# RWKV-7 scan: the order in which four engines take its steps

## The chip, the core and the metric

The kernel runs on one core of a Trainium2 chip. The metric is the device time of one execution in microseconds (us). Engines: TensorE (PE; its weight loads are PEld), VectorE (DVE), ScalarE (ACT), GpSimd (POOL) and SyncE (SP), which issues the DMAs.

## The reference, cut to what matters

A trunk of two layers is run on 128 context tokens and 512 latent tokens with the same weights. The second layer mixes tokens by a bidirectional RWKV-7 scan: 16 heads of 64 channels, a state of 64 x 64 per head and direction.

```python
def rwkv7_scan(r, w, k, v, kk, a, s0):
    def step(s, inp):
        r_t, w_t, k_t, v_t, kk_t, a_t = inp
        sa = jnp.einsum('bhvk,bhk->bhv', s, -kk_t)
        s = s * w_t[:, :, None, :] + sa[..., None] * (kk_t * a_t)[:, :, None, :] + v_t[..., None] * k_t[:, :, None, :]
        return s, jnp.einsum('bhvk,bhk->bhv', s, r_t)
...
    def direction(d, s0):
        w_log = -jax.nn.softplus(-(w0[d] + jnp.tanh(xw @ w1[d]) @ w2[d]).astype(jnp.float32)) - 0.5
        decay = heads(jnp.exp(-jnp.exp(w_log)))
        a = heads(jax.nn.sigmoid((a0[d] + (xa @ a1[d]) @ a2[d]).astype(jnp.float32)))
        kd = k * (1 + (a - 1) * k_a_h)
...
        bonus = jnp.sum(r * kd * r_k_f, axis=-1, keepdims=True) * v
        return y, bonus, s_fin
...
    yn = ((y - mu) * lax.rsqrt(var + LN_X_EPS)).reshape(bsz, n_tok, D_MODEL) * ln_w + ln_b
    out = (yn + (bonus_f + bonus_b).reshape(bsz, n_tok, D_MODEL)) * g
    return out.astype(h.dtype) @ wo, (s_f, s_b)
```

Here kk is the normalised key, mu and var are the mean and variance of y over a head, and g is a gate.

## The kernel before, in words

**Tiling.** Tokens lie along the free dimension (640: 512 latent, 128 context), channels on the 128 partitions, so one tile of 128 channels holds a **pair** of heads. There are 8 pairs, q = 0 to 7. Of a pair the 640 tokens are taken in five **iterations** of 128 tokens (two chunks of 64), both directions at once: iteration n belongs to pair n // 5, and NB = 40 of them run. Within a chunk the recurrence is solved in matrix form, between chunks the state is carried.

**Steps of a chunk solve.** For block m (the work of iteration m, made some iterations ahead):

- G (gram): TensorE makes the products of keys with keys in banks 0 and 1; VectorE masks them out of there (L2490, L2492); GpSimd adds the identity (L2615).
- A1, A2, A3: squares, fourths and eighths of that matrix; ScalarE copies the first two (L2376, L2380), GpSimd adds the identity (L2622), VectorE reads A3 out of the same banks 0 and 1 (L2505, L2506), and the next block's G waits for that.
- GR (read_keys): products of keys with reads in banks 6 and 7, masked by VectorE (L2499).
- B1, B2, B3, B4, B5: the block inverse. ScalarE copies B1 and B2 (L2384, L2388, L2392), VectorE adds B3, B4 and B5 (all L2510). BT turns keys (L2242), ScalarE copies it (L2398). B0 is GpSimd's copy of values (L2641).

**Steps of the walk.** For each of the two chunks of an iteration, s = 0 and 1: x (TensorE, then VectorE's sum L2520), u (TensorE, then ScalarE's copy L2404), s (TensorE, then VectorE's state update L2531, or L2529 where a direction ends; GpSimd prepares its decayed half, L2607, which its table calls x0 and x1). The next chunk's x needs the updated state. y1 is ScalarE's copy of the outputs (L2413); x0 of the next iteration needs it, for the bank.

**Once for a pair.** On ScalarE: decays0 to decays4 (L2370 to L2372, one for each iteration), the sigmoids "prompt", "w", "a" (L2323, L2325), k_square (L2357), k_sum, mean (L2344), var (L2351, L2352), final (L2341), bonus, state (L2335). On VectorE: cum0, cum1 (L2446, L2447), keys0 (L2456, L2460), keys1, keys2, keys3 (L2464, L2467, L2470), staging0 to staging4 (L2476 to L2479), bonus_raw (L2567, L2568), values (L2548), y_sum (L2552), mean (L2541), y_norm0 (L2560, L2561), y_norm1 (L2564), gate (L2544), k_sum (L2451). On TensorE: the head sums of k_sum, mean, var and bonus, the gate product, the transposes of values (L2133), state and final, and the LoRA products of prompt, w and a. These side products share banks 6 and 7 with GR and BT; each waits until the one before it has been read out.

**What sets the order.** Every engine runs its queue in order and waits on semaphores. The order in a queue is written by hand, in one table for each engine: PE_ORDER, DVE_ORDER, ACT_ORDER, POOL_ORDER, and PE_FIRST and ACT_FIRST for the first iteration of a pair (n = 0, 5, ..., 30). run_iteration (from L2033) walks a table for n from -4 to 41. An entry is a step, or a step with an offset:

```python
                what, ahead = entry if isinstance(entry, tuple) else (entry, 0)
                m = n + ahead
```

so ("B5", 0) in iteration n and ("B5", 1) at the end of iteration n - 1 give nearly the same queue. A step that is done once for a pair is in the table of every iteration and runs only when m has the right remainder by 5 (ASIDE and aux). Behind each iteration up to 34 (VectorE: 35) a call of out_ahead_act or out_ahead_dve splits one tile of the next stage's input into a high and a low part (out_high L1144, out_low L1148; six tiles, iterations 29 to 34 on ScalarE, one later on VectorE); in the last iterations the entry "ahead" does that, and on TensorE it runs products of the next stage.

Of the kernel before, what the change touches and what calls it, by code (L numbers as in the profile page):

```python
# [115 lines left out]
def program(nc, a, o):  # L116
    with ExitStack() as ctx:
# [73 lines left out]
        V, A, G = nc.vector, nc.scalar, nc.gpsimd  # L191
# [28 lines left out]
        for l in range(LAYERS):  # L220
            if l == 0:
                ada_stage(0)
                w = a["ab_w_in"][0]
# [241 lines left out]
        fast_x0, x0 = {}, 0  # L465
# [1361 lines left out]
        QD, A1, A2, DD = blocks4(2), blocks4(2), blocks4(3), blocks4(2)  # L1827
# [171 lines left out]
        def place(q, c):  # L1999
# [1 line left out]
            return c if c < 8 else c + 2 * (q % 2)  # L2001


        PE_ORDER = ("var", "mean", "B5", ("final", -1), ("s1", -1), ("GR", 1), ("B1", 1), "x0", ("A1", 2), "bonus", "a", "u0", "state", ("B2", 1), "w", ("A2", 2),
                     "prompt", "s0", ("B3", 1), ("BT", 1), "x1", ("A3", 2), ("values", 1), ("B4", 1), ("gate", 1), ("k_sum", 1), "u1", ("G", 3))
        def with_ahead(order, after):
            return tuple(x for entry in order for x in ((entry, "ahead") if entry in after else (entry,)))

        PE_LAST = {NB - 2: with_ahead(PE_ORDER, ("s0", "x1", "u1")), NB - 1: with_ahead(PE_ORDER, (("s1", -1), "x0", "u0", "s0", "x1", "u1"))}
        PE_FIRST = ("B5", "var", ("s1", -1), ("values", 2), ("GR", 1), ("B1", 1), ("A1", 2), "prompt", ("bonus", 1), "x0", "u0", ("B2", 1), ("A2", 2), "w", "s0", ("A3",  # L2010
                     2), ("a", -1), ("B3", 1), ("k_sum", 1), "x1", ("mean", -1), ("gate", 2), ("BT", 1), ("B4", 1), "final", ("state", 1), "u1", ("G",
                     3))
        DVE_ORDER = (("bonus_raw", -1), "B3", ("staging0", -1), ("x1", -1), ("A3", 1), "values", ("keys1", -1), "B4", "gate", "k_sum", ("G", 2), "mean", ("keys2", -1),
                     ("s1", -1), "B5", ("GR", 1), "y_sum", "x0", "staging3", "staging4", "staging1", "y_norm0", "keys3", ("cum0", -1), ("keys0", 1),
                     "cum1", "staging2", "y_norm1", "s0")
        ACT_FIRST = (("k_square", 2), "prompt", "decays3", "u0", ("A2", 2), ("a", -1), "decays1", ("B2", 1), "w", ("BT", 1), ("decays4", 2), "u1", "y1", ("B1", 2),
                     ("decays0", -1), "var", ("decays2", 2), ("state", 2), ("mean", -1), ("A1", 3), ("final", -1), ("bonus", -1), ("k_sum", 2))

        def first_of_pair(n):
            return n >= 0 and n % 5 == 0 and n + 5 < NB  # L2020

        ACT_ORDER = ("a", "state", "bonus", "u0", ("B2", 1), ("A2", 2), ("k_square", 1), ("decays1", 1), ("BT", 1), "mean", ("decays0", 1), "u1", ("decays3", 1), "w",
                     ("k_sum", 1), "final", ("var", 1), "y1", ("decays2", 1), ("decays4", 1), ("B1", 2), ("A1", 3), "prompt")
        POOL_ORDER = (("A2", 3), ("x1", 1), ("G", 4), ("B0", 3), ("x0", 2), ("A1", 4))

        DVE_LAST = with_ahead(DVE_ORDER, ("staging2",))
        ACT_LAST = with_ahead(ACT_ORDER, (("var", 1),))

# [41 lines left out]
        def rwkv_pe(pe):  # L2070
# [224 lines left out]
            for n in range(-4, NB + 2):  # L2295
                run_iteration(n, PE_FIRST if first_of_pair(n) else PE_LAST.get(n, PE_ORDER), tasks, side)
            for item in LAST_ASIDE:
# [4 lines left out]
        def rwkv_act(act, step):  # L2302
# [118 lines left out]
            for n in range(-4, NB + 2):  # L2421
                run_iteration(n, ACT_FIRST if first_of_pair(n) else ACT_LAST if n >= 35 else ACT_ORDER, tasks, side, aux)
                if n < 35:
# [10 lines left out]
        def rwkv_dve(dve, step):  # L2434
# [145 lines left out]
            for n in range(-4, NB + 2):  # L2580
                run_iteration(n, DVE_LAST if n >= 36 else DVE_ORDER, tasks, side, aux)
                if n < 36:
# [439 lines left out]
```

## Time and profile before

| | us |
|---|---|
| median of 3 runs | 2205.68 |
| lowest and highest run | 2205.41 and 2209.05 |
| the profiled execution, its own time | 2206.71 |
| its span, first to last instruction | 2204.9 |
| TensorE busy in the span | 2048.0 (93%) |
| VectorE, ScalarE, GpSimd busy | 1415.6, 1041.6, 317.6 |
| the scan, from its first staging to its last state update | about 1177 to 1703 |

How to read it: busy time counts an engine's instructions; register, branch, semaphore and DMA-issuing instructions are not in it. Times in rows are us from the span's start. A timeline merges like instructions (x is their count) and tells the idle time of the engine before them, with the work that ended it. PEclk is the granted share of TensorE's clock. An instruction's end overlaps the next one's start by up to 0.1 us.

### The profile page before, as it was taken

To read this page: it belongs to the slowest core of one execution; us is meant where nothing else is said; L and a number is where in the kernel's file an instruction comes from. 1 tells how busy PE (TensorE), PEld (TensorE's weight loads), DVE (VectorE), ACT (ScalarE), POOL (GpSimd) and SP (SyncE) were. 2 spreads that over 40 slices of the span, in tenths; PEclk is the share of its full clock that TensorE was granted. 3 is DMA by queue.
4 is the path that set the end of the run, shared out by engine and by line. 5 is a ranking of instruction groups with operands and counts; after the bars stand their busy time and mean duration, and the time that the engine had idled before them with its cause. 6 is when DMAs were issued, how large, how long until landed. Compare 5 with 4: busy or idle time off the path is not lost. (4 is left out here: it accounts for less than half of the span.)

```text
span 2204.9 us, 60453 instructions
## 1 busy us (share of the span) xinstructions
PE 2048.0 (93%) x26203; PEld 1836.3 (83%) x26203; DVE 1415.6 (64%) x2698; ACT 1041.6 (47%) x1887; POOL 317.6 (14%) x542
## 2 busy tenths in 40 slices
PE   5999877898999999989998899999988999999999
PEld 2689754578999999967997777777777989999999
DVE  2242375655666675777535888888885468585857
ACT  5252354434535343566334566666664264434353
POOL 1000131001000000010002544444442200000000
PEclk8999999999999999999998999999999999999999
DMA  7212205960231323113210000000000221322312
GB/s 281 86 39 79 79 1 213 372 226 20 77 96 58 96 66 107 58 29 115 80 39 8 8 10 7 9 9 10 10 25 25 88 66 58 96 77 77 96 58 87
DMA packets 129764, 167.86 MB, mean 76 GB/s; under 512 B 13900, under 2 KB 87388, under 8 KB 129372
## 3 DMA queue, kind: packets, MB, share of 16 engines
q1 hardware_dynamic: 129500, 164.00, 22.2%
q8 instruction: 208, 3.41, 0.6%
q14 instruction: 56, 0.46, 0.1%
HBM read 160.44 MB, written 3.54 MB: 74 GB/s over the span
## 5 line engine op out<-in xcount | busy, mean ns | idle before, releaser
L178 PE MATMUL psum<-arena 64*64 64x64 f32 (+5 forms) x16064 | 585.6, 240 | 94.8 <-ACT arena L1411 14.8
L178 PEld LDWEIGHTS psum<-arena 64*64 64x64 f32 (+3 forms) x16064 | 464.6, 140 | 231.2 <-issue 99.5
L178 PE MATMUL psum<-hidden_high,weights_high 128*128 128x320 f32 x896 | 277.2, 309 | 0.5 <-DVE arena L1020 0.5
L178 PE MATMUL psum<-hidden_low,weights_high 128*128 128x320 f32 x896 | 276.9, 309 | 0.0
L178 PE MATMUL psum<-hidden_high,weights_low 128*128 128x320 f32 x896 | 276.9, 309 | 0.0
L178 PE MATMUL psum<-norm_high,weights_high 128*128 128x320 f32 x960 | 218.8, 309 | 0.0
L178 PE MATMUL psum<-norm_low,weights_high 128*128 128x320 f32 x960 | 218.8, 309 | 0.0
L178 PE MATMUL psum<-norm_high,weights_low 128*128 128x320 f32 x960 | 218.7, 309 | 0.0
L178 PEld LDWEIGHTS psum<-hidden_high,weights_high 128*128 128x128 f32 x896 | 168.2, 188 | 0.9 <-issue 0.7
L178 PEld LDWEIGHTS psum<-hidden_low,weights_high 128*128 128x128 f32 x896 | 168.2, 188 | 0.0
L178 PEld LDWEIGHTS psum<-hidden_high,weights_low 128*128 128x128 f32 x896 | 168.2, 188 | 0.0
L178 PEld LDWEIGHTS psum<-norm_low,weights_high 128*128 128x128 f32 x960 | 160.5, 188 | 0.0
L178 PEld LDWEIGHTS psum<-norm_high,weights_low 128*128 128x128 f32 x960 | 160.5, 188 | 0.0
L178 PEld LDWEIGHTS psum<-norm_high,weights_high 128*128 128x128 f32 x960 | 160.4, 188 | 0.0
L999 DVE TENSOR_TENSOR hidden<-hidden 128x640 f32<-128x640 f32 x32 | 26.4, 826 | 175.6 <-ACT hidden L946 175.6
L944 ACT ACTIVATE hidden<-psum 128x640 f32<-128x640 f32 x64 | 45.1, 705 | 189.0 <-PE psum L178 189.0
L899 ACT ACTIVATE weights_high<-weight_sums 128x512 fp32r<-128x512 f32 x128 | 76.7, 624 | 106.5 <-DVE weight_sums L918 55.6
L621 POOL TENSOR_TENSOR arena<-arena 128x640 f32<-128x640 f32 x24 | 41.7, 1738 | 568.8 <-ACT arena L613 568.1
L1020 DVE SCALAR_TENSOR_TENSOR arena<-psum,ada,arena 128x128 f32<-128x128 f32 (+2 forms) x208 | 83.4, 430 | 30.1 <-PE psum L178 29.3
L903 DVE TENSOR_TENSOR weights_low<-weight_sums,weights_high 128x512 fp32r<-128x512 f32 x128 | 88.3, 700 | 8.4 <-ACT weights_high L899 8.4
L899 ACT ACTIVATE weights_high<-weights 128x512 fp32r<-128x512 f32 x96 | 58.2, 622 | 68.4 <-PE psum L178 68.4
L2615 POOL TENSOR_TENSOR arena<-arena,constants 64x128 f32<-64x128 f32 x160 | 67.2, 420 | 153.0 <-DVE arena L2490 139.9
(268 smaller groups left out, 3992.9 us busy)
## 6 DMA issues: line engine op xcount, KB each, us to landing
weights<-in_mlp_w SPq DMA_DIRECT2D x64, 1024.0 KB, 5.3
arena<-in_ada_w SPq DMA_DIRECT2D x24, 2048.0 KB, 9.3
arena<-in_ab_w_in SPq DMA_DIRECT2D x6, 2048.0 KB, 7.8
arena<-in_ab_w_out SPq DMA_DIRECT2D x2, 2048.0 KB, 9.0
arena<-in_rwkv_wv SPq DMA_DIRECT2D x2, 2048.0 KB, 8.1
arena<-in_rwkv_wr SPq DMA_DIRECT2D x2, 2048.0 KB, 8.1
arena<-in_rwkv_wk SPq DMA_DIRECT2D x2, 2048.0 KB, 7.9
arena<-in_x_sample SPq DMA_DIRECT2D x1, 2048.0 KB, 10.1
```

Of the source, the lines that this page charges most:

```text
L178: return nc.tensor.matmul(out, lhsT, rhs, start=start, stop=stop, skip_group_check=shared)
L621: G.tensor_tensor(total, a0 if k == 1 else total, (a0, a1)[k % 2], ALU.add).then_inc(S("norm_squares_added"), 1)
L899: A.activation(slots_of(WHI)[:, j], slot_raw(l, grp, i, j), ACT.Copy).then_inc(S("slot_high"), 1)
L903: V.tensor_tensor(slots_of(WLO)[:, j], slot_raw(l, grp, i, j), slots_of(WHI)[:, j], ALU.subtract)\
L944: A.activation(h, PS[:, 2 * j:2 * j + 2, 0:HN], ACT.Relu).then_inc(S("up_evacuated"), 1)
L999: V.tensor_tensor(h[:, H_T1:H_T3 + 1, :], h[:, H_B11:H_B22 + 1:3, :], h[:, H_B12:H_B12 + 1, :].broadcast_to([P, 2, HN]), ALU.subtract)\
L1020: ins = V.scalar_tensor_tensor(x, PS[:, bank, c:c + t1 - t0], gate[:, m, g:g + 1], x, ALU.mult, ALU.add)
L2615: ins = G.tensor_tensor(P1[HALF[h], d, 0], QD[r, h, 0], units(r), ALU.add)
```

## The change

The order tables of TensorE, VectorE, ScalarE and GpSimd are replaced by others. The functions that do the steps, their waits, ASIDE, aux and run_iteration are the same.

```diff
-        PE_ORDER = ("var", "mean", "B5", ("final", -1), ("s1", -1), ("GR", 1), ("B1", 1), "x0", ("A1", 2), "bonus", "a", "u0", "state", ("B2", 1), "w", ("A2", 2),
-                     "prompt", "s0", ("B3", 1), ("BT", 1), "x1", ("A3", 2), ("values", 1), ("B4", 1), ("gate", 1), ("k_sum", 1), "u1", ("G", 3))
+        PE_ORDER = ("prompt", "mean", "var", "B5", ("final", -1), ("s1", -1), ("GR", 1), ("B1", 1), "x0", ("A1", 2), "a", "w", "state", "bonus", "u0", ("B2", 1), ("A2",
+                     2), "s0", ("B3", 1), ("BT", 1), "x1", ("A3", 2), ("B4", 1), ("values", 1), ("k_sum", 1), ("gate", 1), "u1", ("G", 3))
...
-        PE_FIRST = ("B5", "var", ("s1", -1), ("values", 2), ("GR", 1), ("B1", 1), ("A1", 2), "prompt", ("bonus", 1), "x0", "u0", ("B2", 1), ("A2", 2), "w", "s0", ("A3",
-                     2), ("a", -1), ("B3", 1), ("k_sum", 1), "x1", ("mean", -1), ("gate", 2), ("BT", 1), ("B4", 1), "final", ("state", 1), "u1", ("G",
-                     3))
-        DVE_ORDER = (("bonus_raw", -1), "B3", ("staging0", -1), ("x1", -1), ("A3", 1), "values", ("keys1", -1), "B4", "gate", "k_sum", ("G", 2), "mean", ("keys2", -1),
-                     ("s1", -1), "B5", ("GR", 1), "y_sum", "x0", "staging3", "staging4", "staging1", "y_norm0", "keys3", ("cum0", -1), ("keys0", 1),
-                     "cum1", "staging2", "y_norm1", "s0")
-        ACT_FIRST = (("k_square", 2), "prompt", "decays3", "u0", ("A2", 2), ("a", -1), "decays1", ("B2", 1), "w", ("BT", 1), ("decays4", 2), "u1", "y1", ("B1", 2),
-                     ("decays0", -1), "var", ("decays2", 2), ("state", 2), ("mean", -1), ("A1", 3), ("final", -1), ("bonus", -1), ("k_sum", 2))
+        PE_FIRST = (("k_sum", 2), "B5", ("s1", -1), ("final", 1), ("state", 1), ("GR", 1), ("B1", 1), ("A1", 2), "prompt", "x0", "u0", ("B2", 1), ("gate", 2), ("mean",
+                     -1), ("A2", 2), "w", ("bonus", 1), "s0", ("var", -1), ("A3", 2), ("B3", 1), "x1", ("BT", 1), ("B4", 1), "u1", ("values", 2),
+                     ("G", 3), ("a", -1))
+        DVE_ORDER = ("k_sum", "values", ("G", 2), "mean", "B5", ("s1", -1), ("keys2", -1), ("GR", 1), ("keys0", 1), "y_sum", "x0", "staging3", ("cum0", -1), "cum1",
+                     "staging4", "staging1", "y_norm0", "keys3", "staging2", "s0", ("B3", 1), "staging0", ("bonus_raw", -1), "x1", "y_norm1", ("A3",
+                     2), "keys1", ("B4", 1), ("gate", 1))
+        ACT_FIRST = (("decays0", -1), ("decays3", 2), ("y1", -1), ("bonus", -1), ("mean", -1), ("a", -1), ("k_square", 2), ("state", 2), ("B1", 1), ("A1", 2), "decays1",
+                     ("decays4", 2), "prompt", "u0", ("A2", 2), "var", ("final", -1), ("k_sum", 2), ("B2", 1), "w", ("BT", 1), "u1", ("decays2", 2))
...
-        ACT_ORDER = ("a", "state", "bonus", "u0", ("B2", 1), ("A2", 2), ("k_square", 1), ("decays1", 1), ("BT", 1), "mean", ("decays0", 1), "u1", ("decays3", 1), "w",
-                     ("k_sum", 1), "final", ("var", 1), "y1", ("decays2", 1), ("decays4", 1), ("B1", 2), ("A1", 3), "prompt")
-        POOL_ORDER = (("A2", 3), ("x1", 1), ("G", 4), ("B0", 3), ("x0", 2), ("A1", 4))
+        ACT_ORDER = (("y1", -1), "decays2", "decays3", ("B1", 1), ("A1", 2), "a", "decays4", "bonus", "u0", "state", ("B2", 1), ("A2", 2), "mean", ("decays1", 1),
+                     ("k_square", 1), ("BT", 1), "prompt", ("decays0", 1), "u1", ("k_sum", 1), "final", "w", ("var", 1))
+        POOL_ORDER = ("G", ("B0", -1), ("x0", -2), "A1", "A2", ("x1", -2))
```

The tables of the last iterations (PE_LAST, DVE_LAST, ACT_LAST) are made from these. Written out as queues, with the number of the block or iteration behind a step, VectorE's from x0 of iteration 17 to x1 of iteration 20 is

```
before: x0.17 y_norm0 keys3 y_norm1 s0.17 B3.18 staging0 x1.17 A3.19 B4.18 gate G.20 s1.17 B5.18 GR.19 x0.18
        staging1 staging2 s0.18 bonus_raw B3.19 x1.18 A3.20 values B4.19 G.21 s1.18 B5.19 GR.20 x0.19
        staging3 staging4 s0.19 B3.20 x1.19 A3.21 B4.20 k_sum G.22 s1.19 B5.20 GR.21 y_sum x0.20 keys0 s0.20 B3.21 x1.20
after:  x0.17 y_norm0 keys3 s0.17 B3.18 staging0 x1.17 y_norm1 A3.19 B4.18 gate G.20 B5.18 s1.17 GR.19 x0.18
        staging1 staging2 s0.18 B3.19 x1.18 A3.20 B4.19 values G.21 B5.19 s1.18 GR.20 x0.19
        staging3 staging4 s0.19 B3.20 bonus_raw x1.19 A3.21 B4.20 k_sum G.22 B5.20 s1.19 GR.21 keys0 y_sum x0.20 s0.20 B3.21 x1.20
```

In the third iteration of a pair keys2 also goes from ahead of s1 and B5 to behind them. ScalarE's changes in a pair are: y1 of the fourth iteration ahead of decays3, decays4 from ahead of B1 and A1 to behind them, u0 of the fifth iteration ahead of state, and mean ahead of BT.

## Rows read from the trace of the kernel before

**Rows 1.** The page, busy us and share of the span of an engine.

```profile
PE 2048.0 (93%) x26203; PEld 1836.3 (83%) x26203; DVE 1415.6 (64%) x2698; ACT 1041.6 (47%) x1887; POOL 317.6 (14%) x542
```

**Rows 2.** Pair 2: us, PE, PEld, DVE, ACT, POOL, PEclk, DMA share, GB/s.

```profile
1325.00:1388.00 63.00, 57.40 (x1905) 48.23 (x1902) 53.92 (x118) 40.06 (x98) 28.61 (x60) 1.00 0.04 10
```

**Rows 3.** Timeline of VectorE in iteration 12: start us, us, instruction, idle before.

```profile
1358.42 1.14 DVE L2564 TENSOR_TENSOR arena<-arena 128x640 f32<-128x640 f32 x1
1359.60 0.47 DVE L2531 SCALAR_TENSOR_TENSOR arena<-psum,arena 128x64 f32<-128x64 f32 x2
...
1362.35 0.41 DVE L2506 COPY arena<-psum 128x256 f32<-128x256 f32 x1
...
1363.01 0.80 DVE L2544 TENSOR_TENSOR arena<-arena,psum 128x640 f32<-128x640 f32 x1
1363.84 0.69 DVE L2490 TENSOR_TENSOR arena<-psum,constants 128x512 f32<-128x512 f32 x1
...
1366.21 1.29 DVE L2499 TENSOR_TENSOR arena<-psum,constants 128x512 f32<-128x512 f32 x2 [0.28 <-PE psum L178]
```

**Rows 4.** Timeline of TensorE, x1 and what follows, iterations 12 and 17.

```profile
1360.13 4.10 PE L178 MATMUL psum<-arena 64*64 64x64 f32 x124 [1.65 <-DVE arena L2531]
...
1422.73 5.70 PE L178 MATMUL psum<-arena 64*64 64x64 f32 x124 [1.65 <-DVE arena L2531]
```

**Rows 5.** Busy time around two falls of the clock, columns as in rows 2.

```profile
1419.90:1423.30 3.40, 1.75 (x67) 1.48 (x66) 3.30 (x7) 1.96 (x5) 1.39 (x2) 1.00 0.02 5
1423.30:1426.70 3.40, 3.40 (x38) 2.20 (x28) 2.39 (x8) 0.00 (x0) 0.00 (x0) 0.50 0.00 0
...
1488.10:1491.50 3.40, 3.40 (x30) 2.14 (x32) 2.55 (x7) 0.00 (x0) 0.00 (x0) 0.50 0.00 0
```

**Rows 6.** Timeline of VectorE in iteration 13, bonus_raw.

```profile
1371.54 0.82 DVE L2567 TENSOR_TENSOR arena<-arena 128x640 f32<-128x640 f32 x1
1372.39 1.15 DVE L2568 SCALAR_TENSOR_TENSOR arena<-arena,param_cols 128x640 f32<-128x640 f32 x1
```

**Rows 7.** Timeline of GpSimd, the sum behind A2 in iterations 13 and 14.

```profile
1371.57 1.28 POOL L2622 TENSOR_TENSOR arena<-arena,constants 128x256 f32<-128x256 f32 x1 [2.07 <-ACT arena L2380]
...
1383.42 0.64 POOL L2622 TENSOR_TENSOR arena<-arena,constants 128x256 f32<-128x256 f32 x1 [1.54 <-ACT arena L2380]
```

**Rows 8.** Timeline of TensorE in iterations 13 and 14.

```profile
1372.91 0.46 PE L178 MATMUL psum<-arena 64*64 64x64 f32 x16 [0.29 <-POOL arena L2622]
...
1375.85 3.01 PE L178 MATMUL psum<-arena 64*64 64x64 f32 x80 [0.24 <-DVE arena L2510]
1379.14 1.43 PE L178 MATMUL psum<-arena 64*64 64x64 f32 x56 [0.28 <-ACT arena L2413]
```

**Rows 9.** Timeline of ScalarE in iteration 14, decays4 and u0.

```profile
1378.78 0.42 ACT L2370 ACTIVATE arena<-arena 128x256 f32<-128x256 f32 x1
...
1381.08 0.55 ACT L2404 ACTIVATE arena<-psum 64x128 f32<-64x128 f32 x2
```

**Rows 10.** VectorE (B3 sum) and TensorE (k_sum head sums), iteration 14.

```profile
1383.67 0.42 DVE L2510 TENSOR_TENSOR arena<-psum,arena 128x256 f32<-128x256 f32 x1
...
1385.34 1.26 PE L178 MATMUL psum<-arena,constants 64*64 64x320 f32 x8
```

**Rows 11.** Timeline of VectorE in iteration 15, x0, keys0 and s0.

```profile
1392.00 0.29 DVE L2520 TENSOR_TENSOR arena<-psum,arena 128x128 f32<-128x128 f32 x1 [0.23 <-DVE arena L2552]
...
1392.38 1.05 DVE L2460 SCALAR_TENSOR_TENSOR arena<-arena,param_cols 128x640 f32<-128x640 f32 x1
1396.19 0.48 DVE L2531 SCALAR_TENSOR_TENSOR arena<-psum,arena 128x64 f32<-128x64 f32 x2 [2.75 <-PE psum L178]
```

**Rows 12.** Timeline of ScalarE ahead of iteration 0, the state copy.

```profile
1195.27 0.34 ACT L2335 ACTIVATE arena<-psum 128x64 f32<-128x64 f32 x2
```

**Rows 13.** Timelines of VectorE (out_low, iteration 32) and TensorE (B4, iteration 33).

```profile
1615.57 0.82 DVE L1148 TENSOR_TENSOR mixed_low<-arena,mixed_high 128x640 fp32r<-128x640 f32 x1
...
1630.92 1.65 PE L178 MATMUL psum<-arena 64*64 64x64 f32 x64 [0.80 <-DVE arena L2510]
```

## The prediction

> **What bounds the kernel now.** I read the page first: TensorE is busy 93% of the span, the other engines far less [rows 1]. The change touches nothing but the four order tables of the RWKV scan, so the next view is the busy time of stretches of the scan, one pair of heads (five iterations) each: in the 63 us of pair 2 TensorE is at work for 57, VectorE for 54, ScalarE for 40, GpSimd for 29 [rows 2]. A pair therefore ends when TensorE has done its fixed work plus its short stalls, and VectorE has only some 9 us of slack in 63. So I read the timelines of the four engines inside pairs and asked of each stall which read-out it waited for.
>
> **What the change really moves.** An entry of a table is a step and an offset in iterations, and only the resulting row of steps on each queue counts. Written out that way, GpSimd's queue comes out the same, step by step. TensorE's has two swaps in a pair: the second block (B4) ahead of the value transposes, the state transposes ahead of u0. ScalarE's has four in a pair. VectorE's is the one that changes: in each of 39 iterations the third block's sum (B5) goes ahead of the state update s1, and in each pair y_norm1, bonus_raw, values and keys0 change places. In the last pairs the six splits of the next stage's input (out_high, out_low) shift too, since they hang at the end of an iteration. No instruction and no DMA is added or removed; SyncE's queue stays.
>
> **B5 ahead of s1.** TensorE makes B5 before s1, so the sum can run while s1 is still being made: 0.41 us leave VectorE's path. But what follows on VectorE, the KB masking (GR), waits for TensorE anyway (idle 0.28 us ahead of L2499 [rows 3]). I take 0 for all 39; the ends are -0.1 us and, where the state comes later for GpSimd and x0, +0.1 us each: -4 to +4 us over the scan at the very most.
>
> **y_norm1 behind x1.** In the third iteration of a pair VectorE does keys3, y_norm1 (1.14), and only then the state update that starts at 1359.60 [rows 3]; TensorE has idled 1.65 us for it when x1 starts [rows 4]. The update needs nothing of y_norm1, so without it it starts at 1358.42, 1.18 us sooner, and x1 with it. Late next: y_norm1 now stands ahead of the two read-outs of A3, which end at 1362.76 before and at about 1362.7 after. The next Gram product writes the banks that they read. Its own read-out starts at 1363.84, so its 16 matmuls, at 0.46 us [rows 8], started at about 1363.3; they can start at 1362.7 now. That is 0.6 us, of which the gate's read-out (0.80 at 1363.01, now up to 0.1 sooner only), which the final state's transposes wait for, takes another 0.1: just under 0.5 us a pair. Five pairs like this one (iterations 7, 12, 17, 22, 27): -2.4 us. In iteration 32 an out_low moves into the same place, and I count -0.2. The ends: nothing, and the whole 1.18 us in six pairs, -7.1 us.
>
> **The granted clock.** After two of these waits TensorE was granted half: 3.4 us at 0.50 from 1423.3 and from 1488.1, that is the 1.2 of the two levels 1.2 and 2.4 GHz, and in the stretch just before TensorE was busy for 1.75 of 3.40 us [rows 5]. The same 124 matmuls take 4.10 us at full clock and 5.70 in the half-clock case [rows 4]: 1.6 us each, 3.2 together. With x1 sooner the stretch ahead of them is about 1.2 us fuller, and I take it that both are gone: -3.2 us. The ends: 0, and +1.6 for a new one elsewhere. The Trainium skill (TensorE: Matmul & The Clock Gate, "Wait — 56ns, not 53.3ns?") speaks against counting this: the moment at which the chip looks is not tied to the program, so the same kernel shows other numbers of slow matmuls from run to run. By it a drop can return in other pairs and the sum would end 3.2 us higher; the trace leaves that open, since pair 2 had the same 1.65 us wait and no drop.
>
> **bonus_raw an iteration later, values behind B4.** bonus_raw (0.82 + 1.15) stood ahead of B3's sum [rows 6]. It also ran beside GpSimd's identity sum, 1.28 us there against 0.64 elsewhere [rows 7]. TensorE idled 0.29 us for the one and 0.24 us for the B4 sum that came late; 0.28 us later it waits again, for ScalarE's y1, which stood behind decays3 [rows 8] and now comes first. Together 0.8 us of stalls go. ScalarE's decays4 (about 1.2 us from 1378.78) moves from ahead of the A1 read-out to behind it: A1 is copied sooner, but the u copy at 1381.08 now waits for decays4 instead [rows 9], so that is neutral. In its new place, between the B3 sum and x1, bonus_raw takes 2.0 us where TensorE still has BT, x1, A3, B4 and the k_sum head sums to do, until 1386.6, 2.9 us behind the sum's start at 1383.67 [rows 10]; it is hidden there, but slows a GpSimd sum again: +0.2.
>
> **keys0 ahead of x0.** In a pair's first iteration x0's sum starts at 1392.00 and keys0 comes behind it, ending at 1393.43, in front of an idle 2.75 us [rows 11]. Moved ahead of the sum it delays x0 by 1.2 us. The 0.8 us won above, less 0.2, pay half; 0.6 us are left. The stretch behind u0 is held by ScalarE's sigmoids of the prompt, which also start 0.6 us sooner, and by GpSimd; I take the rest as absorbed and count bonus_raw, values, decays and keys0 together at 0 for six pairs. The ends a pair: -0.8 (keys0 hidden) and +1.2 (nothing won before it).
>
> **Start and end.** Ahead of the first x0 ScalarE does decays4 after A1's copy, so the state copy at 1195.27 [rows 12] and all behind it come 0.6 us later: +0.6. In iterations 31 to 35 each out_low (0.82) stood between the state update and B3's sum; TensorE idled up to 0.80 us for B4 there, bonus_raw included [rows 13]. Behind B4 it costs at most the next Gram read-out: -0.6 in sum.
>
> **Sum:** -2.4 - 0.2 - 3.2 + 0 + 0.6 - 0.6 = -5.8 us. Against the profiled execution's own 2206.71 us that is 2200.9; against the median of the runs, 2205.68, which lies 1.0 us lower, 2199.9. I forecast **2200.5 us**. A measurement of this kernel can tell about 0.2% (4.4 us) from no change; its three runs alone lie 3.6 us apart.
>
> **Rivals.**
> 1. The drops of the clock stay, or come elsewhere: only -2.6 us, 2203.5 us. For it: pair 2 with the same wait at full clock. Against: both drops follow exactly this wait. Chance 0.27.
> 2. VectorE's slack is larger than I give it: y_norm1 is fully hidden behind x1 (-7.1) and half of the 0.8 us a pair survives keys0 (-2.4), with the clock's -3.2: -12.7 us, 2193.5 us. For it: TensorE's 1.65 us wait is the largest regular one. Against: rows 3, the A3 read-outs leave only 0.6. Chance 0.14.
> 3. Slower: keys0 ahead of x0. If u0 is what the pair waits for, each first iteration pays 1.2 us (six pairs 7.2, and 0.3 for the first), and if y1 and bonus_raw win nothing before it, only the 2.6 us of y_norm1 stand against it: +0.6 for the start makes +5.5 us, 2211 us by the median, clock as before. It decides from the point where the lead at x0 is under 0.6 us and ScalarE's copy of u0 no longer waits for the sigmoids. For it: VectorE has only 0.23 us of slack ahead of x0's sum, and the 2.75 us come behind it [rows 11], which says that TensorE is the later one. Against: the sigmoids, which the same u0 waits for. Chance 0.11.
> 4. Nothing net: TensorE's fixed 57 us a pair hide every swap, 2206 us. Chance 0.08.
>
> My own case has 0.40. Its times spread over 2198 to 2203 us, so it counts mostly, not wholly, as faster by over 0.2% (under 2201.3 us): faster 0.26 + 0.14 + 0.08 of rival 1 = 0.48, slower 0.11, same 0.41. Since cases of both signs hold much of the chance: the likeliest one's own range is 2198 to 2203. The range of 8 in 10 leaves out the outer half of rivals 2 and 3: 2194.5 to 2209.0 us.
>
> **What the new profile would show.** Right: in third iterations VectorE's state update directly behind keys3, TensorE's idle ahead of x1 at 0.4 to 0.8 us in place of 1.65, y_norm1 behind x1 and a Gram product that waits for L2506; no stretch at 0.50 between 1200 and 1700 us; L2622 at 0.64 beside B3; pairs of 63 us. keys0: x0's sum about 0.4 us later against GR, VectorE's 2.75 us idle down to 1.5. Wrong: u0 starting over 0.6 us later against GR in first iterations with s0 as late (rival 3), a 0.50 stretch in the scan (rival 1), or x1 still waiting, which would say that the state update hangs on something other than VectorE's queue.

## The result, and the profile after

The changed kernel takes 2195.38 us (median of 5 runs, 2192.05 to 2199.47), the kernel before 2207.5 us (5 runs, 2205.41 to 2209.05) beside it: a ratio of 0.9943, with a 95% interval of 0.9931 to 0.9956. It is faster by 0.57%, about 12 us, where I forecast 5. A second set of runs gave 0.9951 (0.9938 to 0.9965). The profiled execution took 2194.96 us against 2206.71, so the two profiles show 11.75 us of it.

From here on the **walk** is the time from the first to the last start of the x sum (L2520). One row for each kernel gives it, from the view of one line's instructions (count; shortest, median, longest ns; first and last start). Before, then after:

```profile
L2520 DVE TENSOR_TENSOR arena<-psum,arena x80: 274/282/293, 1205.3 to 1700.4; 128x128 f32<-128x128 f32 x80
```

```profile
L2520 DVE TENSOR_TENSOR arena<-psum,arena x80: 276/280/293, 1208.0 to 1688.7; 128x128 f32<-128x128 f32 x80
```

495.1 us became 480.7: 14.4 us are won inside the walk. Ahead of it 2.7 us are lost; behind it both kernels take 504.5 us. What became of TensorE's idle time in the walk is in the view of its waits (us in total, times, longest), before:

```profile
PE psum L178 <- DVE arena L2531: 13.1, 12, 1.7
PE psum L178 <- DVE arena L2520: 6.6, 16, 1.1
PE psum L178 <- issue: 6.5, 11, 1.6
PE psum L178 <- POOL arena L2622: 5.7, 15, 1.6
PE psum L178 <- DVE arena L2510: 4.4, 12, 1.0
```

and after:

```profile
PE psum L178 <- DVE arena L2520: 16.4, 19, 1.4
PE psum L178 <- DVE arena L2531: 6.0, 11, 0.7
PE psum L178 <- issue: 3.2, 8, 0.7
...
PE psum L178 <- DVE arena L2506: 2.9, 6, 0.5
...
PE psum L178 <- POOL arena L2622: 1.7, 2, 1.4
PE psum L178 <- DVE arena L2510: 1.0, 1, 1.0
```

The waits for the state update (L2531), for GpSimd's identity sum (L2622) and for the B sums (L2510) shrink by 14.5 us together; those for the x sum (L2520) grow by 9.8, and the A3 read-outs (L2506) appear with 2.9. "Issue", where TensorE waits for nothing that the profile shows, falls by 3.3. Not all of the gain is in such rows: in the walk TensorE's idle time falls by 6.4 us (49.4 to 43.0) and its busy time, with the same 14465 matmuls, by 8.0 (445.7 to 437.7). Of the 8.0, 3.2 are the granted clock; the other 4.8 are short waits that a profile counts as busy.

**y_norm1.** VectorE and TensorE in iteration 12, and TensorE in iteration 17, answer to [rows 3, 4]:

```profile
1357.00 1.68 DVE L2470 TENSOR_TENSOR arena<-arena 128x640 f32<-128x640 f32 x2
1358.72 0.48 DVE L2531 SCALAR_TENSOR_TENSOR arena<-psum,arena 128x64 f32<-128x64 f32 x2
...
1361.14 0.81 DVE L2564 TENSOR_TENSOR arena<-arena 128x640 f32<-128x640 f32 x1
```

```profile
1359.25 3.17 PE L178 MATMUL psum<-arena 64*64 64x64 f32 x76 [0.45 <-DVE arena L2531]
1362.88 1.16 PE L178 MATMUL psum<-arena 64*64 64x64 f32 x48 [0.47 <-DVE arena L2506]
...
1420.73 3.17 PE L178 MATMUL psum<-arena 64*64 64x64 f32 x76 [0.45 <-DVE arena L2531]
```

The state update follows keys3 directly, x1 waits 0.45 us instead of 1.65, and the next Gram product waits 0.47 us for the A3 read-outs. No stretch of the walk is at half clock; before, two were [rows 5].

**The fourth and fifth iterations.** TensorE from one BT (L2242) to the next, iterations 13 and 14, against [rows 8]:

```profile
1371.48 0.46 PE L2242 MATMUL psum<-constants,arena 64*128 64x64 f32 x8
1371.87 1.28 PE L178 MATMUL psum<-arena 64*64 64x64 f32 x56
1373.08 0.77 PE L2133 MATMUL psum<-constants,arena 128*128 128x128 f32 x5
1373.78 4.57 PE L178 MATMUL psum<-arena 64*64 64x64 f32 x168
1378.49 0.45 PE L178 MATMUL psum<-constants,arena 64*64 64x64 f32 x8
1378.77 3.46 PE L178 MATMUL psum<-arena 64*64 64x64 f32 x128
1382.17 0.46 PE L2242 MATMUL psum<-constants,arena 64*128 64x64 f32 x8
```

There is no stall left in it, and it is 10.69 us from BT to BT. The same two steps before:

```profile
1371.64 0.46 PE L2242 MATMUL psum<-constants,arena 64*128 64x64 f32 x8
...
1383.56 0.75 PE L2242 MATMUL psum<-constants,arena 64*128 64x64 f32 x8
```

That was 11.92 us: 1.23 us are won in a pair.

**keys0.** TensorE at x0 of iteration 15, before and then after:

```profile
1392.34 5.13 PE L178 MATMUL psum<-arena 64*64 64x64 f32 x176 [0.47 <-DVE arena L2520]
1397.40 0.46 PE L2242 MATMUL psum<-constants,arena 64*128 64x64 f32 x8
```

```profile
1392.02 4.62 PE L178 MATMUL psum<-arena 64*64 64x64 f32 x176 [1.44 <-DVE arena L2520]
1396.57 0.46 PE L2242 MATMUL psum<-constants,arena 64*128 64x64 f32 x8
```

The wait for the x sum is 0.97 us longer, but the same 176 matmuls take 0.51 us less: a row of merged matmuls holds its short waits as busy time. Moved ahead of x0, keys0 costs 0.46 us, not its own length.

**bonus_raw in its new place.** It stands in the stretch just ahead of that x0, and it isn't free there. TensorE, behind the k_sum head sums of iteration 9, before and then after:

```profile
1323.81 4.38 PE L178 MATMUL psum<-arena 64*64 64x64 f32 x160
```

```profile
1323.31 4.71 PE L178 MATMUL psum<-arena 64*64 64x64 f32 x160
```

The same 160 matmuls take 0.33 us more. From the BT of iteration 9 to that of iteration 10, keys0 included, TensorE takes 13.55 us before (1321.24 to 1334.79) and 14.41 after (1320.68 to 1335.09), so 0.86 of the 1.23 us are given back.

### The profile page after: what moved, and what is told of

Read it like the earlier page. It is cut to its first block, busy times and chain, and to the rows that moved or that the text cites. A ratio compares the mean times of both kernels' runs of the same rounds, so it can differ in the third digit from the quotient of the medians.

```text
span 2193.2 us, 60459 instructions
## 1 busy us (share of the span) xinstructions
PE 2041.7 (93%) x26203; PEld 1834.8 (84%) x26203; DVE 1408.8 (64%) x2698; ACT 1040.2 (47%) x1887; POOL 310.2 (14%) x542
## 4 chain that ended last, share of the span: by engine, by line
PE 76%; DVE 9%; issue 7%; ACT 4%; POOL 2%; DMA 1%; PEld 1%; PEldq 0%; POOLq 0%; DVEq 0%; SPq 0%; ACTq 0%
PE psum L178 74%; ACT arena L1857 1%; DVE arena L2499 1%; ACT arena L1411 1%; DVE arena L2446 1%; PEld psum L178 1%; DMA arena<-in_x_prompt 1%; DVE small L1377 1%; PE psum L1342 0%; DVE arena L2470 0%; PE psum L2242 0%; POOL arena L2615 0%; ACT arena L642 0%; POOL arena L621 0%; DMA arena<-in_ada_w 0%
## 5 line engine op out<-in xcount | busy, mean ns | idle before, releaser
L178 PE MATMUL psum<-arena 64*64 64x64 f32 (+5 forms) x16064 | 575.2, 239 | 88.4 <-DVE arena L2520 16.4
```

Of the source, the lines that this page charges most:

```text
L178: return nc.tensor.matmul(out, lhsT, rhs, start=start, stop=stop, skip_group_check=shared)
```

## The experiments

"Walk" is always that of the profiled execution. Kernels of one session share their runs of the kernel before; its medians were 2211.97, 2212.36 and 2211.02 us in the three sessions, so ratios, not microseconds, are compared across them.

### y_norm1_alone: the kernel before, y_norm1 behind x1

```diff
-        DVE_ORDER = (("bonus_raw", -1), "B3", ("staging0", -1), ("x1", -1), ("A3", 1),
+        DVE_ORDER = (("bonus_raw", -1), "B3", ("staging0", -1), ("x1", -1), ("y_norm1", -1), ("A3", 1),
...
-                     "cum1", "staging2", "y_norm1", "s0")
+                     "cum1", "staging2", "s0")
```

> The kernel before with y_norm1 moved behind x1 and nothing else. The walk is counted from the first to the last start of x's sum (L2520): 495.1 us before, 480.7 after the whole change. Theory (the A3 read-outs behind y_norm1 cap the gain at 0.5 us a pair, and both falls of the clock in the walk hang on this wait): -2.7 us and no 0.50 stretch in the walk, so a walk of 489.2 and -5.9 us in the time. Rival (the clock falls by chance): -2.7 us, with 0.50 stretches still there, a walk of about 492. Second rival (the whole 1.18 us of six pairs is won once nothing else moves): a walk of 484.8 with the clock's share.

Measured: 2203.05 us, ratio 0.9966 (0.9952 to 0.9981), walk 1204.4 to 1694.0 = 489.6 us, 5.5 less. TensorE in iteration 12:

```profile
1357.38 3.17 PE L178 MATMUL psum<-arena 64*64 64x64 f32 x76 [0.48 <-DVE arena L2531]
1361.01 1.16 PE L178 MATMUL psum<-arena 64*64 64x64 f32 x48 [0.47 <-DVE arena L2506]
```

x1 comes 1.17 us sooner (1.65 less 0.48), and the A3 read-outs hold the next Gram product back. What is left of it, from one BT to the next and without the clock, is 0.39 to 0.46 us in each of six pairs, 2.6 us together. The two half-clock stretches, which are gone, are the other 3.2 us: 5.8, where the walk is 5.5 us shorter. Both terms are those of the prediction (2.4 + 0.2, and 3.2).

### y_norm1_back: the kernel after, y_norm1 ahead of s0 again

```diff
-                     "staging4", "staging1", "y_norm0", "keys3", "staging2", "s0", ("B3", 1), "staging0", ("bonus_raw", -1), "x1", "y_norm1", ("A3",
+                     "staging4", "staging1", "y_norm0", "keys3", "staging2", "y_norm1", "s0", ("B3", 1), "staging0", ("bonus_raw", -1), "x1", ("A3",
```

> The kernel after with y_norm1 put back ahead of the state update s0, all else as in the change. Theory: TensorE waits 1.65 us ahead of x1 again in six pairs: walk 480.7 + 2.7 = 483.4, and up to 3.2 more if its clock falls again behind that wait, 486.6. Rival (the gain comes from the other moves, and this wait only shifts): walk within 1 us of 480.7.

Measured: 2206.51 us, ratio 0.9978 (0.9963 to 0.9993), walk 493.3 us, above the forecast's 486.6, with five half-clock stretches, 8 us. Three of them follow this wait. The busy time in windows (columns as in [rows 2]) around one of them:

```profile
1363.10:1366.50 3.40, 1.76 (x55) 1.49 (x53) 3.30 (x7) 1.97 (x5) 1.38 (x2) 0.93 0.04 7
1366.50:1369.90 3.40, 3.40 (x48) 2.43 (x42) 2.38 (x8) 0.00 (x0) 0.00 (x0) 0.57 0.00 0
```

The other two follow the x0 wait that keys0 makes. Without the 8 us the walk is 485.3, 4.6 over that of after: 2.3 for the six waits (from BT to BT) and 2.6 for more issue stalls (5.8 us against 3.2), within 0.3.

### bonus_back: the kernel after, bonus_raw ahead of the B3 sum of the fifth iteration

```diff
-                     ... "s0", ("B3", 1), "staging0", ("bonus_raw", -1), "x1", ...
+                     ... "s0", "bonus_raw", ("B3", 1), "staging0", "x1", ...
```

> The kernel after with bonus_raw back ahead of B3's sum of the fifth iteration, all else as in the change. Theory (its removal there freed the A3 read-out's wait for GpSimd, 0.5 us, and B5's wait, 0.4 us, and its new place costs nothing): 0.9 us in each of seven pairs comes back, walk 487. Rival (what was won there is paid where bonus_raw now stands, in front of x1): walk within 1.5 us of 480.7.

Measured: 2206.52 us, ratio 0.9977 (0.9964 to 0.9991), walk 1204.0 to 1694.2 = 490.2 us, 9.5 more than after, one half-clock stretch of 1.6 us and 1.7 us more of issue stalls (4.9) among them. TensorE in iteration 13:

```profile
1369.26 0.46 PE L2242 MATMUL psum<-constants,arena 64*128 64x64 f32 x8
...
1370.52 0.46 PE L178 MATMUL psum<-arena 64*64 64x64 f32 x16 [0.29 <-POOL arena L2622]
1371.54 0.68 PE L178 MATMUL psum<-arena 64*64 64x64 f32 x16 [0.56 <-DVE arena L2510]
```

The next BT starts at 1381.24, 11.98 us after this one: all of the 1.23 us that the change won there is lost again. bonus_raw alone makes the stretch long, by the two stalls shown (0.85 us) and by what the merged rows hide. The stretch behind it gets shorter: from the BT of iteration 9 to that of iteration 10 it is 14.01 us against 14.41 in after, and the row of 160 matmuls is back at 4.38. So bonus_raw costs 0.40 us in its new place, and 0.9 us a pair is the net. Without the half-clock stretch and the 1.7 us of issue stalls the walk is 486.9, the 487 of the forecast, though the new place does cost something.

### bonus_alone: the kernel before, bonus_raw behind the B3 sum of the next iteration

```diff
-        DVE_ORDER = (("bonus_raw", -1), "B3", ("staging0", -1), ("x1", -1),
+        DVE_ORDER = ("B3", ("staging0", -1), ("bonus_raw", -2), ("x1", -1),
```

> The kernel before, with bonus_raw (1.97 us) moved alone, from ahead of the B3 sum of the fifth iteration of a pair to behind the B3 sum of the next one. Measure: the walk, from the first to the last start of the x sum (L2520), 495.1 us before, 480.7 after, and 490.2 in the kernel after with bonus_raw put back. Theory: bonus_raw is the largest part of what my sum took for absorbed. Putting it back cost the walk 9.5 us (one half-clock stretch of 1.6 us among them), so about 1.1 us a pair in 7 pairs; moved alone it should give most of that: walk 487 to 489, kernel 6 to 8 us faster than before. Rival: it needs ScalarE's y1 and the values swap beside it, since TensorE waits for y1 (0.28 us) and B4 next anyway; then it gives the 0.5 us that I read in the stalls of 0.29 and 0.24, 7 times: walk 491.5. Second rival: keys0 behind x0 (its place before) changes nothing of it, but the half-clock stretches stay or new ones come: 1.6 us each on top.

Measured: 2209.51 us, ratio 0.9983 (0.9966 to 1.0), walk 493.9 us: by its number the forecast of 487 to 489 fell. The local gain is there: from BT to BT it is 1373.44 to 1384.22, 10.78 us in place of 11.92. What hides it is the clock and the issue stalls: four half-clock stretches where the kernel before has two (3.2 us more; two are one long one behind an issue stall of 1.64 us), and 9.2 us of issue stalls against 6.5. Without what exceeds the kernel before in both, the walk would be 488.0.

### act_back: the kernel after with ScalarE's tables of before

```diff
-        ACT_ORDER = (("y1", -1), "decays2", "decays3", ("B1", 1), ("A1", 2), "a", "decays4", "bonus", "u0", "state",
+        ACT_ORDER = ("a", "state", "bonus", "u0", ("B2", 1), ("A2", 2), ("k_square", 1), ("decays1", 1), ("BT", 1), "mean",
...
```

> The kernel after with ScalarE's two tables of the kernel before. Theory: of ScalarE's four moves only y1 ahead of decays3 wins (the 0.28 us wait of TensorE in the fifth iteration), decays4 behind A1 wins nothing within a pair and costs 0.6 us at the start: walk +1.7 to +2.5 us (482.4 to 483.2), start 0.6 us sooner, kernel 1 to 2 us slower than after. Rival: ScalarE's order carries a large part of the 8.8 us that y_norm1 and the clock do not explain, because bonus_raw's gain can only be taken when y1 and A1 come sooner: walk +4 us or more. Other rival: nothing, the y1 wait is replaced by another of the same length: walk within 0.5 us of 480.7.

Measured: 2202.2 us, ratio 0.994 (0.9919 to 0.9961), walk 487.2 us. TensorE in iteration 14:

```profile
1381.39 0.81 PE L178 MATMUL psum<-arena 64*64 64x64 f32 x40 [0.28 <-ACT arena L2413]
```

That is the wait for y1 of [rows 8]: 0.28 us, seven times in the walk, 2.0 us; BT to BT is 1374.87 to 1385.90, 11.03 us. Two half-clock stretches behind the x0 wait make 3.2 us of the 6.5, and 0.8 are issue stalls. So ScalarE's order is worth some 2 us, as expected, and the time does not separate the kernel from after. The start, which I had put 0.6 us sooner with these tables, came later, at 1210.4 against 1208.0.

### low_back: the kernel after, out_low between s0 and the B3 sum

```diff
-                run_iteration(n, DVE_LAST if n >= 36 else DVE_ORDER, tasks, side, aux)
-                if n < 36:
-                    out_ahead_dve(dve, n)
+                run_iteration(n, DVE_LAST if n >= 36 else with_ahead(DVE_ORDER, ("s0",)), tasks, side, aux)
```

> The kernel after with the splits out_low of iterations 30 to 35 put back between the state update s0 and the B3 sum, where they stand before. Theory: each then delays the B3 and B4 sums by 0.82 us where TensorE has at most 0.8 us of lead; I had read 0.6 us in all, and the leads of the two traces show about 0.5 us each at iterations 33 and 35: walk +1 to +2 us (481.7 to 482.7), and up to 1.6 us more if a half-clock stretch comes. Rival: the end of the walk is where most of the unexplained gain sits (the lead grows by 3.9 us from iteration 31 to 36), and out_low is the cause: walk +3 to +4 us. Other rival: nothing, it is hidden: within 0.3 us.

Measured: 2200.3 us, ratio 0.9938 (0.9921 to 0.9954), walk 484.5 us. Of the 3.8 us more, 1.8 are there before the first out_low runs (the BT at 1570.99 stands at 1567.99 in after, and the walk began 1.2 us later). Of the 2.0 us behind it about 1.5 are issue stalls (2.8 us against 1.2). That leaves about 0.5 us, so out_low is a small term, and the rival that it carries the end of the walk falls; its exact size is inconclusive.

### s1_first: the kernel after, s1 ahead of B5

```diff
-        DVE_ORDER = ("k_sum", "values", ("G", 2), "mean", "B5", ("s1", -1), ("keys2", -1),
+        DVE_ORDER = ("k_sum", "values", ("G", 2), "mean", ("s1", -1), "B5", ("keys2", -1),
```

> The kernel after with the state update s1 ahead of the B5 sum again on VectorE, all 39 of them. I predicted 0, between -4 and +4 us. Theory: VectorE idles 0.3 to 0.6 us ahead of GR behind both, so the order of the two is free for TensorE: walk within 0.5 us of 480.7, apart from issue stalls (up to 3 us) and half-clock stretches (1.6 each). Rival: the state that comes 0.41 us sooner lets GpSimd and x0 start sooner, and x0 is what TensorE waits for (16.4 us in 19 waits in the kernel after): walk 2 us or more shorter. Other side: B5's sum later delays TensorE's s1 or GR: walk 2 us or more longer.

Measured beside after_again, the unchanged kernel on the same chip (2198.56 us): 2206.85 us, 12 runs from 2202.85 to 2209.76, ratio 0.9983 (0.9973 to 0.9994). The walk is 1208.3 to 1696.5 = 488.2 us. The one regular difference is in the third iterations. TensorE in iteration 12, after and then s1_first:

```profile
1355.33 3.08 PE L178 MATMUL psum<-arena 64*64 64x64 f32 x128 [0.51 <-DVE arena L2520]
```

```profile
1356.77 3.07 PE L178 MATMUL psum<-arena 64*64 64x64 f32 x128 [0.77 <-DVE arena L2520]
```

VectorE has keys2 (1.3 us) between these two steps and GR there, and in after it runs without a gap to the x sum. With s1 first it waits for TensorE's s1, and the x sum is 0.26 us later:

```profile
1353.21 0.47 DVE L2531 SCALAR_TENSOR_TENSOR arena<-psum,arena 128x64 f32<-128x64 f32 x2 [0.47 <-PE psum L178]
```

Over the walk the waits for the x sum are 1.7 us more (18.1 against 16.4). With issue stalls of 8.0 us against 5.2 in after_again, and one half-clock stretch in each, that is more than the 3.4 us between the two walks (488.2 and 484.8). It does not fill up the 8.3 us between the medians: each profile here is of the fastest execution of its kernel, these two are 6.6 us apart, and 3.9 of that lie ahead of the walk. So my 0 was wrong inside the new order, by 1.7 us in what the profiles show, and the rest is open.

### keys0_behind: the kernel after, keys0 behind x0 again

```diff
-                     ... ("GR", 1), ("keys0", 1), "y_sum", "x0", "staging3", ...
+                     ... ("GR", 1), "y_sum", "x0", ("keys0", 1), "staging3", ...
```

> The kernel after with keys0 back behind x0's sum, all else as in the change. Theory (keys0 ahead of x0 costs: u0 ended 1.0 us later against its own stretch, half of it made up further on): 0.5 us in each of the first iterations 5 to 30 and 0.2 in iteration 0, walk 477.5 and the time 3 us under the changed kernel's. Rival (absorbed behind u0 by the sigmoids, as the prediction had it): walk 480.7 within 0.6.

Measured: 2194.42 us, ratio 0.9929 (0.9906 to 0.9952), walk 480.0 us. TensorE at x0 of iteration 15, starting from the same 1389.80:

```profile
1391.05 5.12 PE L178 MATMUL psum<-arena 64*64 64x64 f32 x176 [0.47 <-DVE arena L2520]
1396.10 0.46 PE L2242 MATMUL psum<-constants,arena 64*128 64x64 f32 x8
```

The next BT is 0.47 us sooner than in after, in six pairs 2.8 us; issue stalls (5.1 us against 3.2) took 1.9 back, so the forecast of 477.5 was not reached. Its four runs lie within 1.4 us; those of the eight sets with the long x0 wait (4 to 12 runs) lie 4.7 to 9.9 us apart. But the ten runs of y_norm1_alone, which has no such wait, lie 7.2 us apart, so the spread is not this wait's alone.

### best1: keys0 behind x0, y_norm1 behind the A3 read-outs

```diff
-                     ... ("GR", 1), ("keys0", 1), "y_sum", "x0", ...
+                     ... ("GR", 1), "y_sum", "x0", ("keys0", 1), ...
...
-                     ... "x1", "y_norm1", ("A3", 2), "keys1", ("B4", 1), ("gate", 1))
+                     ... "x1", ("A3", 2), "y_norm1", "keys1", ("B4", 1), ("gate", 1))
```

> The kernel after with two moves more on VectorE: keys0 behind x0 again, and y_norm1 behind the two A3 read-outs. In the kernel after, the next Gram product idles 0.47 us for the A3 read-outs, which y_norm1 (0.81) stands ahead of. Theory: with y_norm1 behind them that stall goes, and the gate's and Gram's read-outs keep their places, so 0.4 us a pair in 6 pairs on top of keys0 behind x0 (walk 480.0): walk 477.6, kernel about 2.5 us faster than after. Rival: y_norm1 now delays the B4 sum by 0.8 us, TensorE's B5 product waits for that instead and nothing is won: walk 480. Slower side: the delay is larger than the old stall: walk 481 to 482.

Measured: 2197.04 us, ratio 0.9923 (0.9907 to 0.9939), walk 480.4 us, and no gain from y_norm1. TensorE, iteration 12 (one line of the program less, so L2509 is the B sum):

```profile
1362.96 3.63 PE L178 MATMUL psum<-arena 64*64 64x64 f32 x108 [0.47 <-DVE arena L2530]
1366.84 0.68 PE L178 MATMUL psum<-arena 64*64 64x64 f32 x16 [0.24 <-DVE arena L2509]
```

The Gram product no longer waits, but B5 waits for the B4 sum, which y_norm1 delays. The rival's case.

### best2: keys0 and y_sum behind x0, y_norm1 behind the B4 sum

```diff
-                     ("GR", 1), ("keys0", 1), "y_sum", "x0", ... "x1", "y_norm1", ("A3", 2), "keys1", ("B4", 1), ("gate", 1))
+                     ("GR", 1), "x0", "y_sum", ("keys0", 1), ... "x1", ("A3", 2), "keys1", ("B4", 1), "y_norm1", ("gate", 1))
```

> The kernel after with three steps of VectorE moved: keys0 and y_sum (0.82) both behind the x0 sum, and y_norm1 behind the A3 read-outs and the B4 sum, directly ahead of the gate. Theory: in the kernel before this one y_norm1 behind A3 alone took 0.67 us from the stall ahead of the Gram product and gave it back where TensorE then waited for the B4 sum; behind B4 it delays neither, so 0.4 to 0.5 us a pair in 6 pairs stay won. Of the 0.47 us that x0 is still late in a first iteration, half at most survives to the end of the iteration, as the 176 matmuls behind it took 5.12 us in place of 4.62 when they began 0.97 us sooner: 0.2 a pair. Walk: 480.0 less 2.4 less 1.2 = 476.4, if it has about 5 us of issue stalls as its neighbours have; 474.5 with 3.2. Rival: the Gram read-out is VectorE's anyway, which is busy without a gap from 1355 to 1365 us in the kernel after, so nothing is won of y_norm1: walk 479. Kernel 2191 to 2193 against 2194 to 2195.

Measured: 2193.85 us (2191.24 to 2195.54), ratio 0.9923 (0.9911 to 0.9936), walk 481.3 us where I expected 476.4. The kernel after on the same chip has 2196.24 as its fastest run and 0.9951 (0.9938 to 0.9965), so this version beats both other orders, before and after, the latter by 4.7 us or 0.2%. It doesn't do so by y_norm1, and its ratio is no better than the 0.9929 of keys0_behind, so keys0's place is all that the runs show for it. TensorE, iteration 12:

```profile
1359.09 4.10 PE L178 MATMUL psum<-arena 64*64 64x64 f32 x124 [0.47 <-DVE arena L2530]
1363.69 0.45 PE L178 MATMUL psum<-constants,arena 64*64 64x64 f32 x8 [0.51 <-DVE arena L2543]
```

Now the final state's transposes wait for the gate's read-out, which closes a row without a gap on VectorE. Three places for y_norm1 behind x1 give the same time (ratios 0.9929, 0.9923 and 0.9923). VectorE has no gap from 1353.6 to 1365.3 us in this profile, so behind x1 it is its whole work that sets the pace, no single step.

### dve_alone: the kernel before with VectorE's table of after

```diff
-        DVE_ORDER = (("bonus_raw", -1), "B3", ("staging0", -1), ("x1", -1), ("A3", 1), "values", ("keys1", -1), "B4", "gate",
+        DVE_ORDER = ("k_sum", "values", ("G", 2), "mean", "B5", ("s1", -1), ("keys2", -1), ("GR", 1), ("keys0", 1), "y_sum", "x0",
...
```

> The kernel before with VectorE's table of the kernel after, the other three tables as before. Theory: VectorE's moves carry most: y_norm1 and the clock 5.5 us, bonus_raw about 1.0 in 7 pairs, keys0 takes 0.47 back in 6, out_low 1.2; what ScalarE adds is the wait for y1 (2.0 us over the walk): walk 486 to 488, with up to 1.6 more for each half-clock stretch, kernel 5 to 8 us slower than after. Rival: without the swaps of TensorE and ScalarE VectorE's table meets read-outs in the wrong order (values ahead of B4 on TensorE but behind it on VectorE), and the walk is over 492.

Measured: 2199.73 us, ratio 0.9955 (0.9939 to 0.9971), beside 0.9951 for the whole change; walk 1205.0 to 1690.8 = 485.8 us with one half-clock stretch. VectorE's table carries the gain. The other three tables add no more than the measurement can tell: I expected this kernel to be 5 to 8 us slower than after, and it is 1.2 us slower by the medians (2199.73 against 2198.56). The y1 waits of 2.0 us, which I had counted against it, are in its trace.

### after_again: the kernel after, unchanged

> The kernel after once more, unchanged. It asks what of a single profile repeats. TensorE's stalls with no releaser (issue) were 3.2 us in its walk and 4.9 to 9.2 us in the walks of all its neighbours but one. Theory: they are not the kernel's own, so this profile shows 4 to 7 us of them, at other places, and a walk of 482 to 484; half-clock stretches in the walk stay at none. Rival: they are the program's, at its own places: 3.2 us again, walk 480.7 within 0.3.

Measured: 2198.56 us, walk 1204.4 to 1689.2 = 484.8 us. The same program had 5.2 us of issue stalls where its first profile had 3.2, and a half-clock stretch where that had none. Windows and TensorE's timeline around it:

```profile
1388.00:1391.40 3.40, 1.95 (x82) 1.95 (x86) 1.32 (x3) 2.84 (x7) 1.49 (x2) 0.83 0.02 5
1391.40:1394.80 3.40, 3.40 (x82) 1.72 (x76) 0.37 (x2) 2.24 (x5) 0.64 (x1) 0.67 0.03 5
```

```profile
1389.45 6.14 PE L178 MATMUL psum<-arena 64*64 64x64 f32 x176 [1.46 <-DVE arena L2520]
```

It follows the x0 wait of 1.46 us that keys0 makes, and the 176 matmuls of 4.62 us take 6.14. Without the stretch the walk is 483.2, in the expected 482 to 484; the stretch itself was not expected. So two profiles of one program differ by 4.1 us in the walk, and an account of a few microseconds holds only where it names the waits.

## Why the prediction was right, and where it was off

The time lies in the range (2194.5 to 2209.0) and on the likely side, but 5 us under the forecast and outside the likeliest case's own 2198 to 2203. The wait behind y_norm1 and the clock, 5.8 us, came out as priced. The other 6 of the 12 us came from a term that I had put at 0 and from stalls that are at least in part not the change's, so that the range held them is owed to its width. By the steps of the sum, for the walk of 14.4 us:

- **y_norm1, -2.4 - 0.2.** Right in mechanism and size: 2.6 us in six pairs, held by the A3 read-outs as said (y_norm1_alone).
- **The granted clock, -3.2.** Right for the places priced: both drops go with the wait (y_norm1_alone has none, y_norm1_back has three behind it). But keys0 made a new wait of 1.44 us, six times, and drops follow that one in some executions (after_again). That they stay or come elsewhere was rival 1; the first profile has none, the second one, so the full 3.2 is in part luck of the profiled execution. The Trainium skill (TensorE: Matmul & The Clock Gate, "What's actually happening") says of the slow matmuls at a kernel's start that the same kernel shows other numbers of them from run to run (the prediction gave it under the heading that follows there). The two profiles of one kernel agree with it in the walk: none and one.
- **bonus_raw, values, decays and keys0 together, 0.** This is the term that was mis-sized. I had 0.8 us of stalls won in the fourth and fifth iterations, less 0.2 in bonus_raw's new place, and 0.6 lost to keys0. Measured in pair 2 (iterations 10 to 14), where no issue stall is in the way: 1.23 us won from BT to BT, about 0.35 lost in the new place, and 0.5 lost to keys0. That leaves 0.37 us a pair, 2.2 us in six. Two readings failed. I priced bonus_raw at the stalls that the timeline shows, but rows of merged matmuls hid 0.4 us more of it; and I set what keys0 costs equal to what was left over ("the rest absorbed"), where a third row, the longer 176 matmuls behind an earlier start, would have given half of its delay.
- **B5 ahead of s1, 0.** In the profiles right in sum and wrong in reason. From the BT of iteration 11 to that of 12 TensorE takes 12.18 us before and 12.21 after; but the change also puts keys2 behind s1, a move that I did not price, and s1_first shows that B5's new place pays for it: 0.26 us in that iteration. By the medians s1_first is 8.3 us slower than after, twice the 4 us that I had called the very most, and no profile shows where.
- **Start +0.6, end -0.6.** Not seen. The walk started between 1204.0 and 1212.4 us over the fourteen profiles, at 1208.0 and 1204.4 in two of one kernel, so 0.6 us is below what a profile shows; out_low is worth about 0.5 us.
- **Not in the sum at all:** issue stalls, 3.3 us less in the first profile after than in that of before. Half of it is one stall of 1.61 us ahead of 1651.62, which the prediction did not look for. Since the two profiles of one program differ by 2 us in them, at most part of it is the change's.

Together -2.6, -3.2, -2.2 and -3.3 make 11.3 of the 14.4 us; the rest lies in the first pair and behind iteration 24 and was not taken apart. Rival 2 (VectorE's slack larger, 2193.5 us) came closest in time, for half of its reason: not y_norm1, but the 2.4 us that outlive keys0, 2.2 as measured. Rival 3's price for keys0 was 1.2 us a pair, and it fell by the trace: 0.46.

Of the signs that I named, those of y_norm1, the clock and the GpSimd sum came as said. Three did not. A pair takes 61.5 us, not 63 (62.3 before, both from BT to BT in pair 2). At iteration 15 the x sum comes 0.97 us later against GR (3.22 us behind its start, 2.25 before), not 0.4. And VectorE's idle time ahead of s0 grew instead of falling to 1.5, since keys0 had stood behind the x sum and no longer fills that time:

```profile
1395.40 0.48 DVE L2531 SCALAR_TENSOR_TENSOR arena<-psum,arena 128x64 f32<-128x64 f32 x2 [3.43 <-PE psum L178]
```

## What to carry to other kernels

Price a step on a nearly full engine by the span between two fixed instructions of the engine that waits (here BT to BT), not by the stalls that a merged timeline prints: short waits inside its rows count as busy. When a side step is moved past a step of the critical chain, look at the longest single wait that this makes, not only at the sum: here five or six long waits a walk, most of them of 1.4 to 1.65 us, drew stretches of half clock (1.6 us each) in some executions, and the kernels without them had none.

## What the runs showed of the hardware

**Half clock follows long waits, in some of them.** Over the fourteen profiles, stretches at half clock in the walk lie only behind three kinds of waits of TensorE: y_norm1's of 1.63 to 1.68 us, keys0's at x0 of 1.38 to 1.57, and one issue stall of 1.64. keys0's drew 8 of them in eight profiles of six waits each, y_norm1's 7 in three profiles of five. The four kernels without either of the first two (y_norm1_alone, keys0_behind, best1, best2) have none. Length alone does not decide: TensorE's wait for GpSimd (L2622) in iteration 1, of 1.35 to 1.60 us in seven profiles, drew none.

**Issue stalls and transfers.** The largest stall without a releaser stands in the same place, iteration 35, in four kernels (before, y_norm1_alone, bonus_alone, s1_first), with 1.35 to 1.64 us. In before it ends at 1651.62, about 2 us behind the second of two loads of 512 KB. The busy tenths of the 16 DMA engines, in 40 slices: before from 1640 to 1660 us, then after from 1630 to 1640:

```profile
DMA  0037993000000068981000000100000001000000
```

```profile
DMA  0000000000000300037999960000002004798997
```

My guess was that the loads hold up the fetching of instructions. They are not enough for it: in the kernel after the second load stands at the same place of the iteration (7 us behind the BT at 1630.94; before, 6.4 behind the one at 1640.61), and that iteration has no issue stall. act_back is the same. What makes these stalls is open.

**GpSimd beside VectorE.** The identity sum L2622 took 1.28 us beside bonus_raw [rows 7]; with bonus_raw gone from there:

```profile
1371.41 0.63 POOL L2622 TENSOR_TENSOR arena<-arena,constants 128x256 f32<-128x256 f32 x1 [2.07 <-ACT arena L2380]
```

Here the sum ends 0.65 us sooner after its start, and with it goes the 0.29 us stall of TensorE at that place [rows 8]. In bonus_back both are there again: 1.28 us and 0.29. In its new place bonus_raw has GpSimd's L2607 beside it, which takes 0.86 us at 1382.99 against 0.40 in bonus_back.
